# A transformer pair on one core: tiles of the first steps of four stages paired, two sums and a transposition moved, a weight split moved ahead of the first head norm

## The chip, the core and the metric

The kernel runs on one core of one Trainium2 chip (trn2). The metric is the device time of one launch in microseconds (us); a run's time is that of its one core.

## What is computed

The reference chains two blocks over 256 tokens of width 1024, batch 1, one layer each, all in float32. Cut to what matters:

```python
# first block: Mamba-like mixer plus a gated convolution, then a squared-relu MLP
u = rms_norm(x, ln1) * (1 + scale1) + shift1
proj = u @ w_in                     # gates, conv inputs, z, xbc, dt
y = ssd_scan(conv_silu(xbc), softplus(dt), ...) ; y = y * silu(z)
yg = yg * rsqrt(mean(yg * yg) + EPS)            # 8 groups of 256 features
x = x + gate1 * ((sigmoid(gl) * p_conv + sigmoid(gl') * (y @ w_ssm_out)) @ w_o)
u2 = rms_norm(x, ln2) * (1 + scale2) + shift2
x = x + gate2 * (square(relu(u2 @ w_up)) @ w_down)
x = rms_norm(x, final_norm)
# second block: two kinds of attention, then a silu-gated MLP
h = modulate(x); q, k, v = h @ w_in_2 ; q, k = head-wise rms_norm
x = x + g1 * (concat(forget_attention, differential_attention) @ w_out)
x = x + g2 * ((silu(h2 @ w_gate) * (h2 @ w_up)) @ w_down)
```

## The kernel before, in words

The work is a list of 143 steps, numbered from 0, that `plan()` writes down (lines 67 to 152). A step multiplies one weight tile of 1024 rows by 256 columns (8 blocks of 128 rows) with activations that lie transposed in SBUF, features on partitions and 256 tokens in the free dimension. Each weight and each activation is split in a high and a low part, and each product is three matmuls: high by high, high by low, low by high (`product_part`, line 1101). A step has two output blocks of 128 columns, called nb 0 and nb 1, each with a PSUM bank of its own, and so 2 x 8 x 3 = 48 matmuls. Three banks (acc0 to acc2) turn, so that nb 1 of a step takes the bank that nb 0 of the step before it used; a bank is free when VectorE or ScalarE has drained it (`drained`, line 430).

The steps, by kind: xbc 0 to 15, cc/cx/cb 16 to 27, gc/co 28 to 31 and 40 to 43, z 32 to 39, gs/so 44 to 55, wo 56 to 59, up 60 to 75, dn 76 to 91, the attention projections 92 to 104 (dq, dk, fg, dq, dk, fq, fk, fq, fk, dv, dv, fv, fv), o2 105 to 108, gt/u2 109 to 130, d2 131 to 142.

Five engines walk the same list, each with its own loop `for n in range(NS)` and an order written out by hand; they meet through semaphores. The queues around the change:

- **SP** only issues transfers: weight tile n when the low split of tile n-3 is done, and columns of the modulation matrices between them. The change touches none of it.
- **ScalarE** (line 869): at the start of step n it writes the high part of the weight tile of step n+2 (`split_hi`, line 708), then drains banks, squares, takes roots and writes high parts of activations. An inverse root is Ln and Exp, whose function table `log_exp_table` (line 745) loads ahead.
- **VectorE** (line 1534): at the start or the end of a step it writes the low part of a tile, w_lo = raw - w_hi (`split_lo`, line 1377), and drains banks; in the head norms (lines 1671 to 1680) it corrects the root and scales q and k.
- **GpSimd** (line 647): low parts of activations (`lo_part`, line 613), sums of squares (`add_squares`, line 599; the z pairs, line 663), gating.
- **TensorE** (line 1282): the products (`products`, line 1148), and between them the sums of squares over partitions: `x_sum` (line 1048) for the norms of the residual stream, and line 1356 for the z groups; head norms (line 1309), attention scores, transposes (`attn_slot`, line 1227).

Attention work is laid out in slots, two for each step from 92 on: slot 2(n-92)+nb. `S_AT` says in which slot which pair's scores are computed, `T_AT` in which which head's weights are transposed, `PV_AT` where they meet the values:

```python
S_AT = {6: 0, 8: 1, 12: 2, 14: 3, 16: 4, 18: 5, 20: 6, 22: 7}
T_AT = {9: 0, 11: 1, 15: 2, 17: 3, 19: 4, 20: 5, 21: 6, 22: 7, 23: 8, 24: 9, 25: 10, 26: 11}
```

Steps 60 and 109 (and 61, 110 with them) start before the norm ahead of them is known ("late" norms): they multiply unnormed activations, and VectorE scales the result afterwards (lines 1563, 1573). The steps behind them, 62 and 111, use the normed activations as the blocks arrive, of which the last three (N_AHEAD = 5) come late.

Of the kernel before, what the change touches and what calls it, by code (L numbers as in the profile page):

```python
# [193 lines left out]
def build(nc, a, out):  # L194
# [47 lines left out]
    T_AT = {9: 0, 11: 1, 15: 2, 17: 3, 19: 4, 20: 5, 21: 6, 22: 7, 23: 8, 24: 9, 25: 10, 26: 11}  # L242
    PV_AT = {20: (0,), 21: (1,), 22: (2,), 23: (3,), 25: (4, 5), 26: (6, 7), 27: (8, 9), 28: (10, 11)}
    FG = start_of["fg"]
    LO_NB = 1
# [12 lines left out]
    with ExitStack() as ctx, ExitStack() as programs:  # L258
# [186 lines left out]
        SUMS = {0: KB, 1: KB + 1, 2: KB + 2, 4: KB + 3}  # L445
# [9 lines left out]
        def square_used(k):  # L455

            for n, b0, b1 in ((0, 0, KB), (1, KB, 2 * KB), (2, 2 * KB, 4 * KB), (4, 4 * KB, 5 * KB)):
                if b0 <= k < b1:
                    b, x = divmod(k - b0, 2) if n == 2 else (k - b0, 0)
                    if n == 0:  # L460
                        return "xsum_done", b + 1
                    if b == KB - 1:
                        return "xsum_done", SUMS[n]
                    return "sq_added", added_at(n, max(b, 1), x) + 1
# [242 lines left out]
        def _(act):  # L707
# [46 lines left out]
            def x_root(n):  # L754

                act.wait_ge(S("xsum_done"), SUMS[n])
                if n == 2:
                    link(act.activation(mx[:, 0:T], M3[:, T:2 * T], ACT.Ln, bias=eps[:, 1:2], scale=1.0 / D))
                    act.activation(mx[:, 0:T], mx[:, 0:T], ACT.Exp, scale=-0.5).then_inc(S("xroot"), 1)
                    inverse_root(sq[:, 0, :], M4[:, 0:T], D, "xroot")  # L760
# [108 lines left out]
            for n in range(NS):  # L869
# [19 lines left out]
                if zs in (5, 9):  # L889
                    log_exp_table()  # L890
                    act.wait_ge(S("zsum_done"), zs - 1)
                    for bank, _ in Z_BANK[0:2] if zs == 5 else Z_BANK[2:4]:
                        inverse_root(bank[:, :], bank[:, :], 2 * P, "zroot")
# [126 lines left out]
                if n == FG + 2:  # L1020
                    log1p_exp_parts(fgr[:, 1:6, :], fgr[:, 0, :], 1)
                for b in z_blocks(zs):
# [16 lines left out]
        def _(pe):  # L1039
# [7 lines left out]

            def x_sum(n):

                take("M4")  # L1050
                if n == 2:
                    take("M3")
                if n == 0:
                    for i in range(KB):
                        pe.wait_ge(S("xsq"), i + 1)
                        pe.matmul(M4[:, 0:T], ones[:, :], sq[:, i % 4, :], start=(i == 0), stop=(i == KB - 1))\
                          .then_inc(S("xsum_done"), 1)
                else:
# [3 lines left out]
                    if n == 2:  # L1062
                        last_w = sq[:, square_at(n, KB - 1, 1) % 4, :]
                        pe.wait_ge(S("sq_added"), added_at(n, KB - 2, 1) + 1)
                        pe.matmul(M3[:, T:2 * T], ones[:, :], rt[:, 1, :], start=True, stop=False)
                        pe.matmul(M3[:, T:2 * T], eps_ones[:, :], rt[:, 0, :], start=False, stop=False)
                        pe.wait_ge(S("xsq"), square_at(n, KB - 1) + 1)
                        pe.matmul(M3[:, T:2 * T], eps_ones[:, :], last, start=False, stop=False)
                        pe.matmul(M4[:, 0:T], ones[:, :], last, start=False, stop=True)
                        pe.wait_ge(S("xsq"), square_at(n, KB - 1, 1) + 1)  # L1070
                        pe.matmul(M3[:, T:2 * T], ones[:, :], last_w, start=False, stop=True).then_inc(S("xsum_done"), 1)
                    else:
                        pe.wait_ge(S("xsq"), square_at(n, KB - 1) + 1)
                        pe.matmul(M4[:, 0:T], ones[:, :], last, start=False, stop=True).then_inc(S("xsum_done"), 1)
# [205 lines left out]

            jq = 0
            for n in range(NS):
                s = steps[n]
                for nb in range(NB):
                    products(n, nb)
                    if n == SOFT_AT + 2 and nb == 0:
# [60 lines left out]
                zs = n - Z0  # L1347
                if 1 <= zs < 9:
                    g = zs - 1
                    bank, name = Z_BANK[g // 2]  # L1350
                    if g % 2 == 0:
                        take(name)
                    if g in (0, 2):
                        pe.wait_ge(S("exp_done"), HEADS)
                    pe.wait_ge(S("zpair"), zs)
                    pe.matmul(bank[:, g % 2 * T:(g % 2 + 1) * T], ones[:, :], sq[:, 2 * (zs % 2), :], start=True, stop=True)\
                      .then_inc(S("zsum_done"), 1)
                    free[name] = ("f_ready", YS + 4 * (g // 2 + 1))
# [9 lines left out]
        def _(dve):  # L1368
# [165 lines left out]
            for n in range(NS):  # L1534
                s = steps[n]
                if n + 2 < NS and not split_late(n) and s.kind != "xbc" and not adds_tokens(n) and n not in LATE:
# [16 lines left out]
                for nb in range(NB):  # L1553
# [25 lines left out]
                    if s.kind == "xbc":  # L1579
# [11 lines left out]
                        if nb == 0 and n == 2:  # L1591
# [3 lines left out]
                        elif nb == 0:  # L1595
# [46 lines left out]
                    for kind, gate in (("wo", 0), ("dn", 1), ("o2", 2), ("d2", 3)):  # L1642
                        if s.kind == kind and s.last:
# [3 lines left out]
                                                     ALU.add).then_inc(S("x_ready"), 1)  # L1647
                    if s.kind == "up":
# [18 lines left out]
                    prev = steps[n - 1] if n else None  # L1667
                    if nb == 1 and prev and prev.kind in ("dq", "dk", "fq", "fk"):
# [23 lines left out]
                    if split_late(n) and nb == LO_NB:  # L1692
# [85 lines left out]
```

## Time and profile before

| | |
|---|---|
| median of 3 runs | 939.42 us (939.03 to 941.12) |
| the profiled execution's own time | 938.5 us |
| its span | 936.7 us |
| granted TensorE clock, mean over the span | 0.991 |
| PE busy (matmuls) | 896.6 us, 96% |
| DVE (VectorE) busy | 675.7 us, 72% |
| ACT (ScalarE) busy | 543.3 us, 58% |
| POOL (GpSimd) busy | 280.6 us, 30% |
| read from HBM | 200.8 MB, mean 217 GB/s |

PE is TensorE, SPq the queue that issues transfers. Times in a trace are counted from the start of the span. A timeline row has start, duration, engine, line, operation, tiles and count, and in brackets how long the engine had been idle before it and whose result ended that. Matmul rows overlap: one is listed with 0.28 us, but the next starts 0.11 us after it, so stretches are read from starts.

### The profile page before, as it was taken

The numbers are of one execution on the slowest core, as the hardware profiler recorded it, in microseconds if no ns is written. First come the engines' busy times: TensorE is split into PE (matmuls) and PEld (weight loads), VectorE is DVE, ScalarE is ACT, GpSimd is POOL, SyncE is SP. The second block draws the span as 40 slices with busy tenths as digits, with TensorE's granted clock in tenths as the row PEclk, the third lists the DMA queues.
The fourth block names the chain that finished last, engine by engine and source line by source line (L and its number), as shares of the span: only waits on it lengthen the run. The fifth ranks groups of instructions, "written<-read, shape, count | busy, mean of one in ns | idle before, by whom it ended". The sixth has DMA issues, their size and how long they took to land.

```text
span 936.7 us, 17831 instructions
## 1 busy us (share of the span) xinstructions
PE 896.6 (96%) x7390; PEld 864.7 (92%) x7390; DVE 675.7 (72%) x870; ACT 543.3 (58%) x840; POOL 280.6 (30%) x266
## 2 busy tenths in 40 slices
PE   5999999999999999999999999988999889999998
PEld 5899999999998999998999999877888889999998
DVE  5989988887677667848788767678895576755442
ACT  4568655557966764466655444557687674454331
POOL 5500003444377411266654111020003551121100
PEclk9999999999999999999999999999999999999999
DMA  9754555666677578844888887414233348755560
GB/s 366 296 216 155 186 216 200 250 238 252 235 286 258 199 255 297 285 138 150 290 301 291 296 316 282 159 60 166 91 136 133 138 154 300 267 193 200 169 225 23
DMA packets 36112, 203.02 MB, mean 217 GB/s; under 512 B 4928, under 2 KB 6080, under 8 KB 17216
## 3 DMA queue, kind: packets, MB, share of 16 engines
q1 hardware_dynamic: 36032, 201.89, 60.2%
q8 instruction: 58, 0.95, 0.4%
q14 instruction: 22, 0.18, 0.1%
HBM read 200.82 MB, written 1.05 MB: 216 GB/s over the span
## 4 chain that ended last, share of the span: by engine, by line
PE 59%; issue 15%; DVE 12%; ACT 8%; POOL 5%; DMA 1%; SPq 0%; POOLq 0%; ACTq 0%; DVEq 0%
PE acc L1132 53%; ACT w_hi L714 3%; DVE w_lo L1382 2%; DVE ada_w L1440 2%; DVE cv L1585 1%; DMA ada_w<-in_ada_tiles 1%; POOL sq L663 1%; POOL rt L611 1%; POOL ul L617 1%; POOL xs L669 1%; DVE fr L1406 1%; POOL maps L658 1%; PE acc L1097 1%; DVE qk L1680 1%; ACT L994 1%
## 5 line engine op out<-in xcount | busy, mean ns | idle before, releaser
L1382 DVE TENSOR_TENSOR w_lo<-raw,w_hi 128x2048 fp32r<-128x2048 f32 x141 | 322.0, 2284 | 146.8 <-ACT w_hi L714 146.8
L1132 PE MATMUL acc<-uh,w_hi 128*128 128x256 f32 x1320 | 375.5, 285 | 8.0 <-POOL ul L617 5.2
L1132 PE MATMUL acc<-ul,w_hi 128*128 128x256 f32 x1320 | 368.7, 279 | 0.0
L1132 PE MATMUL acc<-uh,w_lo 128*128 128x256 f32 x1320 | 368.7, 279 | 0.0
L714 ACT ACTIVATE w_hi<-raw 128x2048 fp32r<-128x2048 f32 x141 | 266.2, 1888 | 79.7 <-PE acc L1132 79.7
L1132 PEld LDWEIGHTS acc<-uh,w_hi 128*128 128x128 f32 x1320 | 251.3, 190 | 14.6 <-POOL ul L617 5.6
L1132 PEld LDWEIGHTS acc<-ul,w_hi 128*128 128x128 f32 x1320 | 251.0, 190 | 0.4 <-issue 0.2
L1132 PEld LDWEIGHTS acc<-uh,w_lo 128*128 128x128 f32 x1320 | 250.9, 190 | 0.0
L1132 PE MATMUL acc<-hidh,w_hi 128*128 128x256 f32 x432 | 119.2, 276 | 0.0
L1132 PE MATMUL acc<-hidl,w_hi 128*128 128x256 f32 x432 | 119.2, 276 | 0.0
L1132 PE MATMUL acc<-hidh,w_lo 128*128 128x256 f32 x432 | 119.2, 276 | 0.0
L1743 DVE CUSTOM_DVE_ANT_0 colw<-colw,cact,par_all 128x1024 f32<-128x1024 f32 x80 | 116.6, 1464 | 0.4 <-DMA colw<-in_ada_cols 0.4
L617 POOL TENSOR_TENSOR hidl<-fr,hidh 128x256 fp32r<-128x256 f32 x54 | 71.7, 1328 | 122.2 <-ACT hidh L723 122.2
L1132 PEld LDWEIGHTS acc<-hidh,w_hi 128*128 128x128 f32 x432 | 81.1, 188 | 0.0
L1132 PEld LDWEIGHTS acc<-hidl,w_hi 128*128 128x128 f32 x432 | 81.1, 188 | 0.0
L1132 PEld LDWEIGHTS acc<-hidh,w_lo 128*128 128x128 f32 x432 | 81.1, 188 | 0.0
L658 POOL TENSOR_TENSOR maps<-maps 128x384 f32<-128x384 f32 x16 | 21.1, 1317 | 112.8 <-ACT maps L995 112.8
L1585 DVE SCALAR_TENSOR_TENSOR cv<-acc,par_all,cv 128x255 f32<-128x255 f32 (+2 forms) x87 | 41.2, 480 | 4.5 <-ACT cv L915 2.0
L617 POOL TENSOR_TENSOR ycl<-fr,ych 128x256 fp32r<-128x256 f32 x16 | 18.9, 1183 | 83.3 <-ACT ych L723 83.3
L723 ACT ACTIVATE hidh<-fr 128x256 fp32r<-128x256 f32 x54 | 22.2, 411 | 34.3 <-DVE fr L1660 26.9
L1132 PE MATMUL acc<-ych,w_hi 128*128 128x256 f32 x128 | 37.1, 290 | 2.9 <-POOL ycl L617 2.9
L611 POOL TENSOR_TENSOR rt<-rt,sq 128x256 f32<-128x256 f32 x20 | 20.3, 1028 | 60.7 <-ACT sq L742 60.7
(366 smaller groups left out, 1581.0 us busy)
## 6 DMA issues: line engine op xcount, KB each, us to landing
raw<-in_tiles SPq DMA_DIRECT2D x137, 1024.0 KB, 5.2
colw<-in_ada_cols SPq DMA_DIRECT2D x80, 512.0 KB, 5.5
ada_w<-in_ada_tiles SPq DMA_DIRECT2D x8, 1024.0 KB, 17.2
raw<-in_rest SPq DMA_DIRECT2D x4, 768.0 KB, 4.5
cact<-in_c_rows SPq DMA_DIRECT2D x2, 512.0 KB, 4.2
xT<-in_x SPq DMA_DIRECT2D x1, 1024.0 KB, 7.4
first_w<-in_tiles SPq DMA_DIRECT2D x1, 1024.0 KB, 17.2
out<-xT SPq DMA_DIRECT2D x8, 128.0 KB, 3.4
```

The costliest lines, as they stand in the source:

```text
L611: pool.tensor_tensor(rt[:, x, :], first, sq[:, k % 4, :], ALU.add).then_inc(S("sq_added"), 1)
L617: pool.tensor_tensor(lo, uf[:, i, :] if i < YC else fr[:, i % NF, :], hi.bitcast(F32), ALU.subtract).then_inc(S("act_lo"), 1)
L658: pool.tensor_tensor(EXS[q % 4], EXS[q % 4], sc[:, q // 4 % 2, :], ALU.mult).then_inc(S("mul_done"), 1)
L663: pool.tensor_tensor(sq[:, k, :], sq[:, k, :], sq[:, k + 1, :], ALU.add).then_inc(S("zpair"), 1)
L669: pool.tensor_tensor(xs[:, b, :], xs[:, b, :], gt[:, nb, :], ALU.mult).then_inc(S("yz_done"), 1)
L714: act.activation(w_hi[:, n % NHL, 0:s.kts, 0:s.cols], raw_of(n), ACT.Copy)\
L723: act.activation(hi, x, ACT.Copy).then_inc(S("act_hi"), 1)
L1132: ins = pe.matmul(o, l, r, start=(s.k == 0 and i == 0 and not j), stop=(s.last and i == s.kts - 1 and j == 2))
L1382: dve.tensor_tensor(lo, raw_of(n), hi.bitcast(F32), ALU.subtract).then_inc(S("lo_ready"), 1)
L1440: dve.tensor_tensor_reduce(w, w, cact[:, :], 1.0, ada_b[:, c:c + 1], ALU.mult, ALU.add, mod[:, c:c + 1]).then_inc(S("ada_sum"), 1)
L1585: ins = dve.scalar_tensor_tensor(cv[:, i % 2, o:T], ps[:, 0:T - o], ssm_w[:, 32 * tap + fb:32 * tap + fb + 1], cv[:, i % 2, o:T], ALU.mult ...
L1743: dve.tensor_tensor_reduce(w, w, cact[:, :], 1.0, ada_b[:, c:c + 1], ALU.mult, ALU.add, mod[:, c:c + 1]).then_inc(S("col_sum"), 1)
```

## The change

Nine edits. (1) Steps 45, 56, 62 and 111 are "paired": both banks take the first blocks (6, 6, 5 and 5 of them) before either takes the rest. (2) The z group sums on TensorE move from the end of a step to behind nb 0 of the next one, and (3) ScalarE takes the z roots behind the two drains of its step, not ahead of them. (4) Three of the sums of norm 2 move into step 91, ahead of block 6 of nb 1 (`x_sum_ahead`); the sum for ScalarE's first root is finished first and signalled alone. (5) The low split of tile 93 moves on VectorE behind the update of nb 0 in step 91. (6) The low split of tile 95 moves ahead of the first head norm in step 93. (7) Transposition 1 moves from slot 11 to 12. (8) The Ln/Exp table load moves from step 59 to 58 and from 108 to 107. (9) The dt weights' splits move up by one step on ScalarE and by half a step on VectorE.

```diff
-    T_AT = {9: 0, 11: 1, ...
+    T_AT = {9: 0, 12: 1, ...
+    D_LAST = max(n for n in range(NS) if steps[n].kind == "dn")
+    PAIRED = {start_of["wo"]: KB - 2, first["so", 0, 0]: KB - 2, U0 + 2: N_AHEAD, G0 + 2: N_AHEAD}
...
# ScalarE
-                if n == 2:
+                if n == 1:
                     act.wait_ge(S("dt_in"), 16)
                     act.activation(dt_hi[:, :, :], dt_raw[:, :, :], ACT.Copy).then_inc(S("dt_hi"), 1)
-                if (s.kind, s.j) in (("wo", 3), ("dn", 3), ("o2", 3)) and s.last:
+                if (s.kind, s.j) in (("wo", 2), ("dn", 3), ("o2", 2)) and s.last:
                     log_exp_table()
...
-                if zs in (5, 9):           # ahead of the loop over nb
+                if zs in (5, 9):           # behind it
                     log_exp_table()
                     act.wait_ge(S("zsum_done"), zs - 1)
...
# TensorE
+            def x_sum_ahead():
+
+                take("M4")
+                take("M3")
+                pe.wait_ge(S("sq_added"), added_at(2, KB - 2) + 1)
+                pe.matmul(M4[:, 0:T], ones[:, :], rt[:, 0, :], start=True, stop=False)
+                pe.matmul(M3[:, T:2 * T], eps_ones[:, :], rt[:, 0, :], start=True, stop=False)
+                pe.wait_ge(S("sq_added"), added_at(2, KB - 2, 1) + 1)
+                pe.matmul(M3[:, T:2 * T], ones[:, :], rt[:, 1, :], start=False, stop=False)
...
+                elif n in PAIRED:
+                    if nb == 0:
+                        for i0, i1 in ((0, PAIRED[n]), (PAIRED[n], KB)):
+                            for b in range(NB):
+                                for i in range(i0, i1):
+                                    product_part(n, b, i)
                 elif size == 1:
                     for i in range(steps[n].kts):
+                        if n == D_LAST and nb == NB - 1 and i == KB - 2:
+                            x_sum_ahead()
                         product_part(n, nb, i)
...
                     products(n, nb)
+                    if nb == 0 and 2 <= n - Z0 < 10:
+                        z_sum(n - Z0 - 2)
...
# VectorE
-                if n + 2 < NS and not split_late(n) and ... and n not in LATE:
+                if n + 2 < NS and not split_late(n) and ... and n not in LATE and n != D_LAST:
                     split_lo(n + 2)
...
-                        if nb == 0 and n == 2:
+                        if nb == 1 and n == 1:
                             dve.wait_ge(S("dt_hi"), 1)
                             dve.tensor_tensor(dt_lo[:, :, :], ...
...
+                    if n == D_LAST and nb == 0:
+                        split_lo(n + 2)
...
+                    if n == I0 + 1 and nb == LO_NB:
+                        split_lo(n + 2)
                     if nb == 1 and prev and prev.kind in ("dq", "dk", "fq", "fk"):
...
-                    if split_late(n) and nb == LO_NB:
+                    if split_late(n) and n != I0 + 1 and nb == LO_NB:
                         split_lo(n + 2)
```

No instruction is added or removed but for the order: the same sums, splits, products and table loads are issued, and the same transfers.

## Rows read from the trace of the kernel before

**Rows 1.** The page, busy time, share and instructions of each engine.

```profile
PE 896.6 (96%) x7390; PEld 864.7 (92%) x7390; DVE 675.7 (72%) x870; ACT 543.3 (58%) x840; POOL 280.6 (30%) x266
```

**Rows 2.** Waits of PE: who waited, for whom; total us, times, longest us.

```profile
PE m L1356 <- POOL sq L663: 3.4, 2, 2.3
PE m L1061 <- POOL rt L611: 3.1, 2, 2.3
```

**Rows 3.** Windows: us, then busy (instructions) by engine, PEclk, DMA share, GB/s.

```profile
536.06:579.58 43.52, 43.52 (x386) 43.52 (x385) 30.08 (x28) 18.43 (x17) 5.86 (x7) 1.00 0.84 304
297.28:300.69 3.41, 3.41 (x19) 3.41 (x18) 2.70 (x3) 1.89 (x3) 3.41 (x3) 0.50 0.97 381
```

**Rows 4.** Timeline of PE, the instruction behind each idle stretch (445.59: none).

```profile
56.14 0.30 PE L1319 MATMUL m<-uh,dt_hi 128*32 128x256 f32 x1 [1.38 <-DVE dt_lo L1593]
...
83.45 0.36 PE L1132 MATMUL acc<-uh,w_hi 128*128 128x256 f32 x1 [0.58 <-DVE cv L1585]
...
296.16 0.70 PE L1356 MATMUL m<-sq,ones 128*128 128x256 f32 x2 [2.25 <-POOL sq L663]
...
399.12 0.38 PE L1132 MATMUL acc<-ych,w_hi 128*128 128x256 f32 x1 [2.91 <-POOL ycl L617]
...
437.13 0.52 PE L1132 MATMUL acc<-uh,w_hi 128*128 128x256 f32 x1 [1.92 <-POOL ul L617]
...
445.59 0.30 PE L1132 MATMUL acc<-uh,w_hi 128*128 128x256 f32 x1
...
602.28 0.67 PE L1061 MATMUL m<-rt,ones 128*128 128x256 f32 x2 [0.77 <-POOL rt L611]
...
625.32 1.13 PE L1309 MATMUL m<-sq,blk 128*128 128x512 f32 x2 [2.02 <-DVE maps L1671]
...
629.89 0.39 PE L1132 MATMUL acc<-uh,w_hi 128*128 128x256 f32 x1 [2.04 <-DVE w_lo L1382]
...
653.75 0.55 PE L1256 MATMUL m<-ident,cct 128*128 128x128 f32 x3 [2.68 <-DVE cct L1494]
...
763.93 0.39 PE L1132 MATMUL acc<-uh,w_hi 128*128 128x256 f32 x1 [2.48 <-POOL ul L617]
```

**Rows 5.** Timeline of DVE around the dt weights, steps 1 to 3.

```profile
55.67 0.42 DVE L1593 TENSOR_TENSOR dt_lo<-dt_raw,dt_hi 128x256 fp32r<-128x256 f32 x1
...
58.49 1.52 DVE L1585 SCALAR_TENSOR_TENSOR cv<-acc,par_all,cv 128x255 f32<-128x255 f32 x3 [0.98 <-ACT cv L915]
```

**Rows 6.** Timelines of ACT, DVE and POOL around steps 37 and 38.

```profile
284.79 1.28 ACT L747 ACT_TABLE_LOAD   x1
...
292.97 2.56 DVE L1382 TENSOR_TENSOR w_lo<-raw,w_hi 128x2048 fp32r<-128x2048 f32 x1 [2.29 <-ACT w_hi L714]
...
293.62 2.49 POOL L663 TENSOR_TENSOR sq<-sq 128x256 f32<-128x256 f32 x1 [0.24 <-ACT sq L887]
```

**Rows 7.** Timeline of DVE, the drain of step 62.

```profile
445.03 0.75 DVE L1652 TENSOR_TENSOR fr<-acc,gt 128x256 f32<-128x256 f32 x2
```

**Rows 8.** Timelines of DVE, POOL and ACT at the end of step 91.

```profile
598.12 2.29 DVE L1382 TENSOR_TENSOR w_lo<-raw,w_hi 128x2048 fp32r<-128x2048 f32 x1 [1.95 <-ACT w_hi L714]
...
601.41 1.41 POOL L611 TENSOR_TENSOR rt<-rt,sq 128x256 f32<-128x256 f32 x2 [17.95 <-ACT sq L742]
...
605.34 0.47 ACT L758 ACTIVATE mx<-m,eps 128x256 f32<-128x256 f32 x1 [2.46 <-PE m L1071]
```

**Rows 9.** Timeline of DVE in the attention stage, steps 94 to 98.

```profile
631.92 0.88 DVE L1680 SCALAR_TENSOR_TENSOR qk<-qk,par_all,rt 128x256 f32<-128x256 f32 x2
...
652.54 0.25 DVE L1714 COPY dta<-exb 128x16 f32<-128x16 f32 x2
...
661.94 0.55 DVE L1513 SCALAR_TENSOR_TENSOR maps<-dist_ts,m 128x384 f32<-128x384 f32 x1 [1.95 <-PE m L1246]
```

**Rows 10.** Timelines of ACT and POOL around the late norm of step 109.

```profile
746.17 1.28 ACT L747 ACT_TABLE_LOAD   x1
...
761.13 4.12 POOL L617 TENSOR_TENSOR ul<-fr,uh 128x256 fp32r<-128x256 f32 x3 [1.37 <-ACT uh L723]
```

More of the change, by code:

```diff
@@ L1021, in _ @@
                     log1p_exp_parts(fgr[:, 1:6, :], fgr[:, 0, :], 1)
+                if zs in (5, 9):
+                    log_exp_table()
+                    act.wait_ge(S("zsum_done"), zs - 1)
+                    for bank, _ in Z_BANK[0:2] if zs == 5 else Z_BANK[2:4]:
+                        inverse_root(bank[:, :], bank[:, :], 2 * P, "zroot")
                 for b in z_blocks(zs):
@@ L1057, in x_sum @@
                           .then_inc(S("xsum_done"), 1)
+                elif n == 2:
+                    last, last_w = (sq[:, square_at(2, KB - 1, x) % 4, :] for x in range(2))
+                    pe.wait_ge(S("xsq"), square_at(2, KB - 1) + 1)
+                    pe.matmul(M3[:, T:2 * T], eps_ones[:, :], last, start=False, stop=False)
+                    pe.wait_ge(S("xsq"), square_at(2, KB - 1, 1) + 1)
+                    pe.matmul(M3[:, T:2 * T], ones[:, :], last_w, start=False, stop=True).then_inc(S("xsum_done"), 1)
+                    pe.matmul(M4[:, 0:T], ones[:, :], last, start=False, stop=True).then_inc(S("xsum_done"), 1)
                 else:
@@ L1061, in x_sum @@
                     pe.matmul(M4[:, 0:T], ones[:, :], rt[:, 0, :], start=True, stop=False)
[L1062 to L1074, printed above, removed]
+                    pe.wait_ge(S("xsq"), square_at(n, KB - 1) + 1)
+                    pe.matmul(M4[:, 0:T], ones[:, :], last, start=False, stop=True).then_inc(S("xsum_done"), 1)
                 free["M4"] = ("xroot", ROOT[n] + (n == 2))
@@ L1279, in attn_slot, with z_sum @@
                         free["M0"] = ("oroot", c + 1)
+            def z_sum(g):
+                bank, name = Z_BANK[g // 2]
+                if g % 2 == 0:
+                    take(name)
+                if g in (0, 2):
+                    pe.wait_ge(S("exp_done"), HEADS)
+                pe.wait_ge(S("zpair"), g + 1)
+                pe.matmul(bank[:, g % 2 * T:(g % 2 + 1) * T], ones[:, :], sq[:, 2 * ((g + 1) % 2), :], start=True, stop=True)\
+                  .then_inc(S("zsum_done"), 1)
+                free[name] = ("f_ready", YS + 4 * (g // 2 + 1))
             jq = 0
@@ L1346, in _ @@
                         free["M4"] = ("fcum_done", 2)
[L1347 to L1358, printed above, removed]
                 if s.kind == "dn" and s.j == 3 and s.last:
@@ L1535, in _ @@
                 s = steps[n]
-                if n + 2 < NS and not split_late(n) and s.kind != "xbc" and not adds_tokens(n) and n not in LATE:
+                if n + 2 < NS and not split_late(n) and s.kind != "xbc" and not adds_tokens(n) and n not in LATE and n != D_LAST:
                     split_lo(n + 2)
@@ L1594, in _ @@
                                .then_inc(S("dt_lo"), 1)
-                        elif nb == 0:
+                        if nb == 0 and n != 2:
                             split_lo(n + 3 if n < 2 else n + 2)
```

16 lines of the change are left out of this document (6 added, 10 removed).

## The prediction, as put on record before the changed kernel was run

> **What bounds the kernel now.** I read the page's busy line first: TensorE's matmuls cover 896.6 us, 96% of the span, no other engine passes 72% [rows 1]. So nothing a slower engine does counts unless TensorE waits for it. The changed kernel issues the same matmuls; time can come only from two places. One is TensorE's idle stretches, which the view of waits and the timeline name one by one [rows 2, 4]. The other is the clock. In the windows view eight whole up steps (8 x 48 matmuls) take 43.52 us at granted clock 1.00, which is 2.4 GHz: 0.1133 us a matmul, 2.72 us for one output block, 5.44 for a step. In a window of 3.41 us the clock is 0.50, 1.2 GHz [rows 3]: half the work is done, so such a stretch costs 1.7 us. There are five of them, one soon behind each of the stalls that end at 296.16, 399.12, 437.13, 653.75 and 763.93 (2.25, 2.91, 1.92, 2.68, 2.48 us) [rows 4]. Three others of like length (2.02 and 2.04 [rows 4], and the 2.3 us one of the second line of [rows 2]) have none behind them; nor has any stall of 0.6 to 1.4 us. So of eight stalls of 1.9 us or more five were followed by a slow stretch, and I price a stall left at that length with about half of 1.7 us extra.
>
> **Part by part, against the profiled execution** (938.5 us; the median of the runs, 939.4, is 0.9 above it).
>
> *dt weights.* The stall of 1.38 us for dt_lo goes. But step 8 waits for VectorE's convolution chain all the same (0.58 us, for cv), and that chain gets later: the low split (0.42 us) now stands ahead of the convolution of step 2, whose start VectorE awaited 0.98 us [rows 4, 5]. What is gained at 56 us is lost at 64 to 83 us, and about 0.3 more: **-0.3**. Bounds: gain 1.4 (the chain has slack), loss 0.4 (the whole split).
>
> *z sums and roots.* The two z waits are 3.4 us together, the longer 2.3 [rows 2], so the first is 1.15; its sum moves half a step (2.72 us) later and the wait goes. For the second, GpSimd adds the squares at 293.62, 8.83 us after ScalarE's table load at 284.79 began [rows 6]. The roots now start behind the drains, 2.7 us later, but the load of a second table (1.28) and two silus (0.7, my reading) no longer stand inside the path: it takes about 6.9, so the add begins at 294.4, and under w_lo it takes 2.49 us as now. It ends near 296.8. TensorE, which stood there from 293.91 on (296.16 - 2.25), comes 2.72 later, less most of the 1.15, near 295.7, and waits 1.1 in place of 2.25; behind 1.1 us no slow stretch has come. At 296.8 it is at a point that it reached at 296.16 + 2.72 = 298.9 before: 2.1, and 1.7 for the slow stretch, **+3.8**; bounds 2.1 (the slow stretch stays) to 4.2 (two stalls and the stretch less no more than 0.9 of rest).
>
> *wo, step 56.* Both banks take six blocks first. 18 matmuls x 0.1133 = 2.04 of the 2.91 us are covered, 0.9 remains, and the slow stretch goes: 2.04 + 1.7 = **+3.7**; bounds 2.0 (the slow stretch stays) to 3.7. Moving the table load from step 59 to 58 gives 0: the chain of norm 1 begins at the last product of 59, and the load was done by then.
>
> *up, step 62.* 15 matmuls = 1.70 of the 1.92 us would be covered. But nb 1 of step 63 takes the bank of nb 0 of step 62, which VectorE drains from 445.03 on, about 0.4 us of the pair listed [rows 7], and TensorE starts there at 445.59 with no wait [rows 4]. VectorE's drain stands in its queue behind the late norm's work, which doesn't move. If TensorE arrives 1.9 us plus the vanished slow stretch sooner, it stands at that bank for some 2.5 us. The idle time moves from block 5 to step 63: **+0.1**, bounds +0.1 and -1.7 (before, the slow stretch lay under this cover; a new one behind the new stall would not).
>
> *Step 91, three sums and split 93.* In the trace GpSimd adds at 601.41, 0.70 each [rows 8], TensorE waits 0.77, and the root's first operation is at 605.34 [rows 4, 8]. The inputs of the first sum come near 599.3. But the split of tile 93 now starts about there and takes its 2.29 us; GpSimd's adds with VectorE in a split took 2.49 us, without it 0.70 [rows 6, 8]. So held, the first add ends near 602.2, as now, but TensorE waits for it *inside* step 91 from 600.8 on (1.4 us), then does three sums (1.4) and six products (0.7), and the last bank, which the last squares need, is ready at 604.7 and no longer at 601.5; the root comes at 606.9. **-1.5**; bounds +0.35 (GpSimd isn't held) and -1.5. The Trainium skill, "GPSIMD Engine Reference", Key points, has a rule that speaks against this edit: GpSimd shares its SBUF interfaces with VectorE and contends with instructions that have two SBUF inputs, as a split has. By that rule the lower bound holds; by the free add of 0.70 the upper would.
>
> *Split of tile 95.* The w_lo stall of 2.04 us goes, for the split comes before the head norm. But the chain of that norm, through the scaling of q and k at 631.92 (0.88 us for two) [rows 9], is what the scores of slot 6 await, and it gets no earlier; it gets the 2 us of split ahead of it instead. The stall of 2.02 us for the distance maps grows to about 2.5. **+0.15**; bounds +0.4, -0.5.
>
> *Transposition 1.* It waits 2.68 us for cct in slot 11. The next thing in that slot is the forget sums, which wait for VectorE's copies at 652.54, 0.7 us earlier [rows 9]. So the stall falls to 1.95. Behind it VectorE is full, and its only pause is 1.95 us before 661.94 [rows 9]: what TensorE wins beyond that it would wait again. 0.7 or more of stall, the slow stretch's 1.7, capped by 1.95 + 0.2: **+2.1**, bounds 1.3 and 2.4.
>
> *gt, step 111, and the load in step 107.* The load (1.28 us) leaves the path of the root, so what follows, with GpSimd's ul at 761.13, comes 1.28 sooner [rows 10]; pairing covers 1.70. Together 2.98 exceed the 2.48 us stall, and nb 1 of step 112 needs a bank that ScalarE drains early. 2.48 + 1.7 = **+4.2**; bounds 2.5 and 4.4. The 2.3 us stall for rt just before stays: it waits for GpSimd behind a split.
>
> Pairing step 45, with all its blocks there, changes nothing: **0**; what hides it is that both its banks come free over 1 us ahead.
>
> *Sum.* -0.3 + 3.8 + 3.7 + 0.1 - 1.5 + 0.15 + 2.1 + 4.2 = 12.2 off 938.5: 926.3. By the count of stalls above, one slow stretch is likely behind the new 2.5 us stall at step 63 (1.7), and half of one behind the other long ones (0.9): **929.0**. The forecast's own range is 926.3 to 931.5.
>
> **Rivals.** *Stalls pass downstream* at 56 or 111 as at 62: a drain or a low part behind the paired step becomes the bound. For: 62 shows the mechanism. Against: in both, the next bank's drain is early. 933 with one lost, 936.9 with both. Chance 0.18. *Nothing held, no slow stretch:* GpSimd's add in step 91 falls beside no split (+1.8 us) and the 0.50 stretches all go: 924.5 to 926. For: every stall but one or two falls under 2.2 us. Chance 0.12. *z roots behind the drains delay ScalarE's high splits:* w_hi of steps 39 to 41 is 2.7 us later, and w_lo with it; VectorE already awaited w_hi 2.29 us at 292.97 [rows 6]. Then the z gain is lost and 0.7 more: 933.5. Chance 0.08. *Slower:* the clock. The change turns five stalls with a slow stretch into about twelve of 0.9 to 2.5 us. If each of those is followed by 3.41 us at 0.50, it costs 12 x 1.7 = 20.4 on 926.3: 946.7; with eight it is 939.9, level with before. Place: behind steps 38, 56, 63, 91, slots 6 and 11, and the norms. Against: none of the stalls up to 1.4 us had one. Chance 0.04. The Trainium skill, "TensorE: Matmul & The Clock Gate", Part 1, says the gate's observation is free-running, so that one kernel's slow stretches differ from run to run; by that the half-stretches above are a chance, not a rule, and no run here has shown it. *The change doesn't do what it says*: for dt, step 62 and split 95 that is already the forecast.
>
> **Numbers.** Forecast 0.58, the rivals 0.18, 0.12, 0.08 and 0.04. A measurement here tells about 0.2%, 1.9 us, from no change. The range 925.5 to 935.0 takes in the forecast, most of the lucky case, the late z splits and one gain lost downstream; 936.9 and the slower side stay out. Faster than 937.5: 0.91; within: 0.04; slower than 941.3: 0.05.
>
> **What would show it.** Right: a stall of about 1.1 us for sq at the z sums; 0.9 for ycl in step 56; none for ul in 62 but 2.5 for a drain in 63; 1.4 for rt inside step 91 and mx 1.5 us later after it; no w_lo stall at 95 but one for the head norm's qk; about 1.95 in slot 11; none in 111; slow stretches two rather than five. Wrong: more of them than four, a stall in 57 or 112, or VectorE's idle time in steps 94 to 99 larger than before.

## The result, and the profile after

| | before | changed |
|---|---|---|
| median of the first comparison | 939.22 us (936.88 to 941.12, 4 runs) | 927.88 us (927.08 to 930.13, 4 runs) |
| ratio, 95% interval | | 0.9884 (0.9856 to 0.9913) |
| the profiled execution's own time, its span | 938.5, 936.7 | 927.08, 925.3 |
| mean granted clock over the span | 0.991 | 0.996 |

Forecast were 929.0 us, 925.5 to 935.0. A second comparison gave 928.38 us (6 runs), ratio 0.9903 (0.9878 to 0.9928). The first line below is the page's busy line of the changed kernel, to be read against [rows 1].

```profile
PE 890.7 (96%) x7390; PEld 858.2 (93%) x7390; DVE 678.6 (73%) x870; ACT 543.0 (59%) x840; POOL 289.4 (31%) x266
```

The instruction counts are the same. TensorE is busy 5.9 us less with the same matmuls: most of that is half-speed stretches, three fewer at 1.7 us each. GpSimd is busy 8.8 us *more* with the same additions. That is no more work either; it is waiting inside an instruction, which a page counts as busy, and it turns out to be the thread of this case.

The view of waits of the changed kernel, TensorE's own (who waited, for whom; total us, times, longest), answers to [rows 2]:

```profile
PE m L1305 <- POOL sq L665: 2.8, 3, 1.3
PE m L1080 <- POOL rt L613: 2.5, 1, 2.5
PE m L1339 <- DVE maps L1693: 2.4, 1, 2.4
PE acc L1140 <- DVE fr L1672: 2.3, 1, 2.3
PE m L1372 <- DVE dta L1736: 1.8, 1, 1.8
```

And TensorE's timeline of the changed kernel, the instruction behind each idle stretch, answers to [rows 4] (start, duration, engine, line, operation, in brackets the idle time before it and what ended it):

```profile
64.59 0.31 PE L1355 MATMUL m<-ident,gt 32*128 32x32 f32 x2 [1.24 <-ACT gt L1005]
...
297.03 0.48 PE L1305 MATMUL m<-sq,ones 128*128 128x256 f32 x1 [1.27 <-POOL sq L665]
...
311.05 0.48 PE L1305 MATMUL m<-sq,ones 128*128 128x256 f32 x1 [1.09 <-POOL sq L665]
...
396.62 0.38 PE L1140 MATMUL acc<-ych,w_hi 128*128 128x256 f32 x1 [0.87 <-POOL ycl L619]
...
438.56 0.38 PE L1140 MATMUL acc<-uh,w_hi 128*128 128x256 f32 x1 [2.26 <-DVE fr L1672]
...
595.28 0.45 PE L1056 MATMUL m<-rt,ones 128*128 128x256 f32 x1 [1.41 <-POOL rt L613]
...
619.74 0.70 PE L1339 MATMUL m<-sq,blk 128*128 128x512 f32 x1 [2.41 <-DVE maps L1693]
...
646.64 0.28 PE L1372 MATMUL m<-dta,tri 128*128 128x8 f32 x1 [1.78 <-DVE dta L1736]
```

Nothing is left at block 5 of step 111 (2.48 us before), nothing at w_lo of tile 95 (2.04), and step 56 waits 0.87 in place of 2.91. New are 1.24 us for gt in step 5, where the gain on the dt weights goes (step 4 ends 1.15 us sooner, step 5 no sooner), 2.26 at a drain in step 63, 1.41 inside step 91, and 1.09 at a third z sum (step 41). The five half-speed stretches are two, in the windows of the changed kernel (columns as in [rows 3]; the clock is the third number from the end):

```profile
621.24:624.44 3.20, 3.20 (x17) 2.62 (x16) 1.69 (x4) 2.26 (x3) 0.00 (x0) 0.50 0.63 264
648.20:651.83 3.63, 3.63 (x19) 3.63 (x18) 3.50 (x8) 1.15 (x2) 0.00 (x0) 0.53 0.00 0
```

To find where 11.4 us of span went, I took the start of the last matmul of every step in both traces and looked where their difference changes (minus is sooner; "pace" is the time from one matmul to the next at full clock, see the last section):

| steps | change in us | edit and what is in it |
|---|---|---|
| 0 to 33 | +0.2 | dt weights |
| 34 to 41 | -1.8 | z sums and roots |
| 42 to 45, 57 to 59 | -1.5 | the pace of the matmuls; pairing step 45 shows nothing |
| 56 | -3.7 | pairing, and no half-speed stretch |
| 60 to 63 | -0.1 | pairing: 2.65 won in step 62, 2.51 lost in 63 |
| 91, 92 | +0.9 | sums ahead, split 93 (+1.3), pace (-0.4) |
| 93 to 98 | -1.1 | split 95, transposition |
| 99 to 110 | -0.3 | waits and pace |
| 111 to 113 | -4.1 | pairing, table load, no half-speed stretch (-4.5), pace (+0.4) |

### The profile page after: what moved, and what is told of

The parts are those of the page before. It is cut to its first block, busy times and chain, and to the rows that moved or that the text cites. A ratio compares the mean times of both kernels' runs of the same rounds, so it can differ in the third digit from the quotient of the medians.

```text
span 925.3 us, 17831 instructions
## 1 busy us (share of the span) xinstructions
PE 890.7 (96%) x7390; PEld 858.2 (93%) x7390; DVE 678.6 (73%) x870; ACT 543.0 (59%) x840; POOL 289.4 (31%) x266
## 4 chain that ended last, share of the span: by engine, by line
PE 63%; issue 14%; DVE 11%; POOL 5%; ACT 5%; DMA 1%; SPq 0%; ACTq 0%; POOLq 0%; DVEq 0%
PE acc L1140 55%; ACT w_hi L716 2%; DVE w_lo L1400 2%; DVE ada_w L1458 2%; DVE cv L1603 2%; POOL rt L613 1%; DMA ada_w<-in_ada_tiles 1%; PE m L1140 1%; PE m L1225 1%; POOL ysl L619 1%; DVE qk L1702 1%; POOL maps L660 1%; POOL ul L619 1%; PE acc L1105 1%; DVE maps L1696 1%
## 5 line engine op out<-in xcount | busy, mean ns | idle before, releaser
L613 POOL TENSOR_TENSOR rt<-rt,sq 128x256 f32<-128x256 f32 x20 | 23.2, 1173 | 55.5 <-ACT sq L744 55.5
L1664 DVE SCALAR_TENSOR_TENSOR xT<-acc,mod,xT 128x256 f32<-128x256 f32 x31 | 14.4, 480 | 32.0 <-PE acc L1140 32.0
```

Of the source, the lines that this page charges most:

```text
L613: pool.tensor_tensor(rt[:, x, :], first, sq[:, k % 4, :], ALU.add).then_inc(S("sq_added"), 1)
L1664: dve.scalar_tensor_tensor(xT[:, b, :], ps, GATE[gate][:, b:b + 1], xT[:, b, :], ALU.mult, ALU.add).then_inc(S("x_ready"), 1)
```

## The experiments

Twelve kernels were run, each beside the kernel before on its chip; the first seven once each. I read those by the starts of the steps in their traces, which repeat to some 0.1 us where neither a half-speed stretch nor the pace differs, and not by their single times (928.7 to 937.6 us).

**Step 56 paired alone.**

```diff
 kernel before
+    PAIRED = {start_of["wo"]: KB - 2}
```

> The kernel before with step 56 alone paired. My theory: pairing covers 18 matmuls, 2.04 us, so the stall at block 6 falls from 2.91 to about 0.9 and the end of step 56 comes 2.0 us sooner, and 3.7 us sooner if no half-speed stretch follows. The changed kernel showed 3.66 us. A rival reading of those 3.66 us is that the stretch at half speed went by chance and would be back in this run: then 2.0. In either case the time between matmuls in steps 57 to 59, 0.1178 us before, is the open point: if it hangs on what happened in step 56 it is 0.1133 as in the changed kernel, and 0.2 us a step are gained more.

```profile
399.16 0.38 PE L1133 MATMUL acc<-ych,w_hi 128*128 128x256 f32 x1 [0.87 <-POOL ycl L618]
```

The wait is 0.87 and no half-speed stretch follows; step 56 ends 3.66 us sooner, to the hundredth what the changed kernel gained there. Steps 57 to 59 went at 0.1133 us a matmul, for 0.64 us more.

**Step 62 paired alone.**

```diff
 kernel before
+    PAIRED = {U0 + 2: N_AHEAD}
```

> The kernel before with step 62 alone paired. My theory: the stall of 1.92 us for ul goes and comes back in step 63 at its second bank, for VectorE's drain, shortened by nothing: 1.7 to 2.0 us there, the end of step 63 is within 0.3 us of before, apart from the half-speed stretch (1.7 us) that may or may not follow it. Rival: pairing covers 1.7 us for good, and step 63 ends 1.7 us sooner.

```profile
444.66 0.39 PE L1133 MATMUL acc<-uh,w_hi 128*128 128x256 f32 x1 [2.27 <-DVE fr L1659]
```

Step 62 ends 2.34 us sooner and step 63 gives 2.51 back: nothing is won, and no half-speed stretch stands in either step. The wait in step 63 is longer than the 2.0 us expected. The wait has moved from block 5 to the drain that stands behind VectorE's split of tile 64.

**Sums of norm 2 and split 93 back in their old places.**

```diff
 changed kernel
-                        if n == D_LAST and nb == NB - 1 and i == KB - 2:
-                            x_sum_ahead()
-                    if n == D_LAST and nb == 0:
-                        split_lo(n + 2)
... (and `x_sum` does all sums of norm 2 again, as in the kernel before)
```

> The changed kernel with the three sums of norm 2 and the split of tile 93 back in their old places. My theory: these two edits cost 1.3 us (root 1.3 us later in the changed kernel), so without them step 92 starts 1.3 us sooner relative to the end of step 90. Rival (what the edit seems made for): they bring the root forward, and without them it comes later.

The root's first operation (ScalarE's timeline), in this kernel:

```profile
600.88 0.47 ACT L760 ACTIVATE mx<-m,eps 128x256 f32<-128x256 f32 x1 [2.46 <-PE m L1073]
```

and in the changed one:

```profile
599.72 0.47 ACT L760 ACTIVATE mx<-m,eps 128x256 f32<-128x256 f32 x1 [0.82 <-PE m L1075]
```

They must be counted from the start of step 91, which is at 591.44 in the first trace and 588.96 in the second: 9.44 and 10.76 us. The kernel before has 9.44 too (595.90 to 605.34 [rows 8]). The two edits cost 1.32 us at the root, and step 92 starts 1.32 later by the same count (14.50 against 13.18 us).

**Sums ahead, split 93 behind the last update.**

```diff
-                    if n == D_LAST and nb == 0:
+                    if n == D_LAST and nb == NB - 1:
                         split_lo(n + 2)
```

> The changed kernel with the split of tile 93 behind the update of the second half of step 91 and not of the first; the three sums stay ahead. My theory: GpSimd's first addition is held 1.5 us only because VectorE splits beside it. Without a split beside it both additions take 0.7 to 0.75 us each, TensorE waits 0 to 0.3 us in place of 1.41 us, and the root's first operation comes 1.4 to 1.7 us sooner than in the changed kernel. Rival: the additions are long for another reason (their own length, or the squares late), and the wait stays near 1.4 us. If the split then runs late, step 92 starts late: a wait for w_lo of tile 93 would show it.

GpSimd's two additions here (POOL's timeline), with no split beside them:

```profile
595.07 1.42 POOL L613 TENSOR_TENSOR rt<-rt,sq 128x256 f32<-128x256 f32 x2 [16.44 <-ACT sq L744]
```

and in the changed kernel, with VectorE's split beside them:

```profile
592.28 2.28 DVE L1400 TENSOR_TENSOR w_lo<-raw,w_hi 128x2048 fp32r<-128x2048 f32 x1
```

```profile
592.95 2.88 POOL L613 TENSOR_TENSOR rt<-rt,sq 128x256 f32<-128x256 f32 x2 [16.43 <-ACT sq L744]
```

The same two instructions take 1.42 us or 2.88. TensorE's wait of 1.41 us in step 91 is gone, the root comes 9.30 us after the start of step 91 (600.39 - 591.09), and step 92 waits for no w_lo. So the hold explains the loss. The whole trace of the changed kernel says the same: 54 of GpSimd's two-input 128x256 instructions (TENSOR_TENSOR) start while a split runs, and each ends 0.5 to 0.6 us after that split; the 32 with no instruction of VectorE beside them take 0.65 to 0.75 us. This run also shows what the sums ahead are worth when nothing is held: 9.44 - 9.30 = 0.14 us, since TensorE pays for the three sums before its last bank instead of behind it.

**Second table load back in step 108.**

```diff
-                if (s.kind, s.j) in (("wo", 2), ("dn", 3), ("o2", 2)) and s.last:
+                if (s.kind, s.j) in (("wo", 2), ("dn", 3), ("o2", 3)) and s.last:
```

> The changed kernel with the second table load back in step 108 (step 111 stays paired). My theory: the load is worth 1.28 us on the root's path and pairing 1.70 us, and only the sum exceeds the stall of 2.48 us. Without the moved load a stall of 0.8 to 1.2 us for ul is back at block 5 of step 111, and step 111 ends 0.8 to 1.3 us later. Rival: pairing alone covers all, because its second bank starts on blocks that are there; then no stall and no change.

```profile
760.19 0.38 PE L1140 MATMUL acc<-uh,w_hi 128*128 128x256 f32 x1 [0.86 <-POOL ul L619]
```

As expected, 0.86 us is back. Step 111 ends 1.46 later, a little more than the 1.3 expected: blocks 6 and 7 come late too and cost some 0.3 us each. Pairing alone doesn't cover this stall; with the earlier load it does.

**Split of tile 95 back behind the head norm.**

```diff
-                    if n == I0 + 1 and nb == LO_NB:
-                        split_lo(n + 2)
-                    if split_late(n) and n != I0 + 1 and nb == LO_NB:
+                    if split_late(n) and nb == LO_NB:
                         split_lo(n + 2)
```

> The changed kernel with the split of tile 95 back behind the first head norm. My theory: that edit is worth about 0.15 us: the stall of about 2.0 us for w_lo of tile 95 is back, the one for the head norm falls from 2.4 to about 2.0, and the wait for q and k in slot 6 (1.61 us in the run without a half-speed stretch here) goes. The end of step 95 moves by 0.5 us or less, apart from the half-speed stretch. Rival: the edit removed one of two waits for good, and the end of step 95 comes 1.5 to 2 us later without it.

```profile
619.32 0.70 PE L1339 MATMUL m<-sq,blk 128*128 128x512 f32 x1 [2.00 <-DVE maps L1691]
...
623.88 0.39 PE L1140 MATMUL acc<-uh,w_hi 128*128 128x256 f32 x1 [2.06 <-DVE w_lo L1400]
```

Two waits of 2.00 and 2.06 us here; with the edit, in the run with split 93 last, 2.38 for maps and then this one for q and k:

```profile
627.69 0.38 PE L1260 MATMUL m<-qk 64*128 64x128 f32 x2 [1.61 <-DVE qk L1702]
```

4.06 us against 3.99. From the end of step 92 to that of 95 it is 18.46 us here, with a half-speed stretch in step 95, and 16.67 there with none. The kernel before has the two waits of this one and no stretch, and takes 16.80: the edit is worth 0.1 to 0.2, the stretch 1.7. The rival's wait "removed for good" has come out as another wait.

**Transposition 1 back in slot 11.**

```diff
-    T_AT = {9: 0, 12: 1, ...
+    T_AT = {9: 0, 11: 1, ...
```

> The changed kernel with transposition 1 back in slot 11. My theory: TensorE waits 2.5 to 2.7 us for cct there and then nothing for the forget sums, so 0.7 to 0.9 us more stall by the end of step 98; the half-speed stretch is there or not. Rival: VectorE is full up to step 99, so the waits add up to the same and the end of step 99 is within 0.2 us.

```profile
651.26 0.33 PE L1272 MATMUL m<-ident,cct 128*128 128x128 f32 x1 [2.68 <-DVE cct L1512]
```

2.68 us for cct, where the changed kernel has 1.78 for dta; step 98 ends 0.89 later and step 99 0.80, where the rival allowed 0.2. Each of the two has a half-speed stretch behind it.

**Four splits held back or moved.** If splits hold GpSimd, and drains stand behind splits, then four edits on VectorE alone should pay:

```diff
+                if 6 <= n - Z0 < 9:
+                    dve.wait_ge(S("zpair"), n - Z0)
-                ... and n not in LATE and n != D_LAST:
+                ... and n not in LATE and n not in (D_LAST, U0 + 2):
                     split_lo(n + 2)
...
-                    if n == D_LAST and nb == 0:
+                    if n == D_LAST and nb == NB - 1:
                         split_lo(n + 2)
...
+                    if n == U0 + 2 and nb == NB - 1:
+                        split_lo(n + 2)
...
+                if (s.kind, s.j) == ("o2", 3):
+                    dve.wait_ge(S("sq_added"), added_at(4, KB - 2) + 1)
                 if adds_tokens(n):
                     split_lo(n + 2)
```

> The changed kernel with four more edits: VectorE's splits in steps 38 to 40 wait until GpSimd has added the z squares of that step; the split of tile 93 stands behind the last update of step 91; the split of tile 64 stands behind both drains of step 62; the split of tile 110 waits until GpSimd has made the last addition of norm 4. My theory (GpSimd is held by VectorE's splits, and drains stand behind them): the z waits of 1.27, 0.4 and 1.09 us fall to under 0.3 together (2.2 to 2.5 us), 1.4 us less stall in step 91 (1.1 to 1.4 us net), 2.26 us in step 63 falls to under 0.4 (1.9 us), and 2.52 us at the sum of norm 4 falls to 0.7 to 0.9 (1.7 us). In all 6.5 to 7.5 us faster than the changed kernel, near 921. Rivals: the postponed splits make TensorE wait for w_lo in steps 40 to 42, 64 and 110 (waits of 1 us and more with w_lo named), then 3 us or less; or the half-speed stretches take it back.

926.92 us (4 runs), ratio to before 0.9872 (0.9841 to 0.9902): against the changed kernel not to be told apart, and far from the 921 expected. By the trace three of four did what was expected: the wait in step 63 is gone (-1.98 us), steps 91 and 92 have 1.4 us less, and the sum of norm 4 waits 0.70 and not 2.52 (-1.83). But TensorE's and GpSimd's rows show what came of it:

```profile
317.09 0.39 PE L1140 MATMUL acc<-uh,w_hi 128*128 128x256 f32 x1 [1.46 <-DVE mc L1653]
...
752.52 0.38 PE L1140 MATMUL acc<-uh,w_hi 128*128 128x256 f32 x1 [1.68 <-POOL ul L619]
```

```profile
749.73 3.44 POOL L619 TENSOR_TENSOR ul<-fr,uh 128x256 fp32r<-128x256 f32 x2 [1.37 <-ACT uh L725]
```

In steps 38 to 41 1.5 us was won, and 1.8 lost in step 42, for a drain behind the postponed split. And the 1.83 of norm 4 came back in step 111, doubled by a half-speed stretch (3.4 us): the low part of block 5 starts at 749.73 beside the split of tile 112 (from 749.60), and the two low parts take 3.44 us, where 0.75 each would do.

**The changed kernel again, a corrected order, and filled waits**, on one chip:

> The changed kernel again, beside the two below on the same chip: 928 us within 1.5. Its idle stretches are the same to 0.1 us; the half-speed stretches need not be. My theory is that these come only behind idle stretches of TensorE of 1.6 us or more and that chance decides behind which: two to four of them, not all in the places of the first profile (behind the waits in steps 94 and 97). Rival: they are fixed to the places of the first profile.

928.38 us, 926.57 to 932.23. The waits are as before; the half-speed stretches now stand behind the waits in step 63 (2.28 us) and at the sum of norm 4 (2.31), and none is in steps 94 to 99. The rival, fixed places, falls.

```diff
 the kernel with four splits moved
-                if 6 <= n - Z0 < 9:
+                if n - Z0 in (6, 7):
                     dve.wait_ge(S("zpair"), n - Z0)
+                if n == start_of["wo"]:
+                    dve.wait_ge(S("act_lo"), MG + KB)
...
                         x_norm(LATE_NORM[LATE[n] // 2], N_AHEAD, KB)
+                        if s.kind == "gt":
+                            dve.wait_ge(S("act_lo"), U4 + N_AHEAD + 1)
                         split_lo(n + NHL)
```

> The four further edits with three corrections: VectorE waits for GpSimd's z addition only in steps 38 and 39 (in step 40 the wait made its drain late and cost 1.46 us in step 42); the split of tile 58 waits until GpSimd has written the last low part of the activations of step 56; the split of tile 112 waits until GpSimd has written the low part of block 5. My theory, GpSimd held by splits: against the changed kernel 1.3 to 1.7 us less in steps 39 to 42, 0.87 in step 56, 2.0 in step 63, 1.1 in steps 91 and 92, 1.8 at the sum of norm 4, and the 1.68 us wait that came back in step 111 of the run with four edits stays under 0.3: 7 to 7.5 us, near 921, if as many half-speed stretches come. Rival: what is gained at the sum of norm 4 comes back in step 111 or 112 by another wait, as it did in that run (3.4 us with the half-speed stretch): then near 924.

```profile
310.68 0.61 PE L1305 MATMUL m<-sq,ones 128*128 128x256 f32 x1 [2.43 <-POOL sq L665]
...
754.46 0.45 PE L1140 MATMUL acc<-uh,w_hi 128*128 128x256 f32 x1 [2.06 <-POOL ul L619]
```

926.16 us, ratio 0.9875 (0.9849 to 0.9901), not the 921 expected. Step 56 has no wait left (-1.16 with what follows), as expected. But without the wait in step 40 the z addition of that step is held, for a wait of 2.43 us, and the split of 112, let go after block 5, now holds block 6: 2.06. Both corrections moved the hold by one instruction. Its trace has four half-speed stretches, two of them behind these waits, and the clock is 0.993 to 0.996 in its six runs.

```diff
 the kernel above
+            def fill(count):
+                take("M4")
+                for _ in range(count):
+                    pe.matmul(M4[:, 0:T], ones[:, :], tri[:, :], start=True, stop=True)
...
+                    if nb == 0 and n == FG:
+                        fill(5)
...
+                    if n == FG + 1 and nb == 0:
+                        fill(3)
...
+                        fill(3)
                         pe.wait_ge(S("nlf_done"), 1)
```

> The same with 11 extra products of constants (0.43 us each, into a bank that is rewritten before it is read) ahead of the three long waits that are left in the attention stage: 5 in step 94, 3 ahead of the scores in slot 6, 3 ahead of the forget sums. They compute nothing that is used. My theory, a half-speed stretch needs TensorE idle before it: with the waits filled to under 0.5 us each there is none in steps 94 to 99 in any run, and the clock over the span is 0.998 or more; the time falls by 1.7 us for each stretch that the kernel without them has there, and by nothing where it has none. Rival: the clock doesn't hang on these waits, and stretches come there as before; or the extra products delay the scores by up to 0.6 us where they outlast the wait.

924.20 us (923.65 to 926.01, 5 runs), ratio 0.9857 (0.9833 to 0.9881), 2.0 us under the kernel without them on the same chip (924.56 to 928.23). The clock is 0.996 to 0.998 in the five runs, one of them under the 0.998 expected; in the trace there is no stretch in steps 94 to 99, where the unfilled kernel has two. The filled kernel ends step 94 1.65 us sooner and the second half of step 95 at the same time (628.37 against 628.30): there TensorE must wait for q and k in any case, so that a half-speed stretch in step 94 costs nothing. The one in step 98 costs 1.4. The trace gives one more stretch less, in step 111 (from the end of step 109 to that of 112 19.51 us against 20.87), and that is not the work of the fills: none stands there, and the wait before it is 2.24 us, so it was chance. The wait of 2.43 us in step 41 isn't filled either and has a stretch behind it in both.

**The last order.** The z waits are left out, the split of tile 112 waits for all three late blocks, and the fills stay:

```diff
-                if n - Z0 in (6, 7):
-                    dve.wait_ge(S("zpair"), n - Z0)
...
-                            dve.wait_ge(S("act_lo"), U4 + N_AHEAD + 1)
+                            dve.wait_ge(S("act_lo"), U4 + KB)
```

> The kernel with the extra products, without the waits for the z additions, and with the split of tile 112 held back until GpSimd has written all three late blocks (in the two runs before, it started between blocks 5 and 6, and GpSimd's low part of block 6 took 2.85 us beside it, for a wait of 2.06 and 2.24 us in step 111). My theory: steps 39 to 42 are as in the changed kernel (two waits of 1.27 and 1.1 to 1.3 us, 1.4 us less than with the waits for z) and no half-speed stretch there; the wait in step 111 is under 0.3 us, and 0.5 to 1 us comes back in step 112 as a wait for w_lo of that tile, since the split ends near 1.5 us later. In all 2 to 3.5 us less than 924.2: 921 to 922. Rival: VectorE's drains behind the split of 112 are late in turn, and all of the 2.2 us comes back in steps 112 and 113: then 922.5 to 924.

922.18 us (921.88 to 923.41, 5 runs), ratio to before 0.9815 (0.9792 to 0.9838), the best of all. It ran on another chip than the two kernels before it, and the intervals of the ratios overlap by a little, so the step from 924.20 is less sure than each kernel's gain on the kernel before. Spans and clocks of the last three:

```profile
core 0: 924.8 us, clock 0.993
```

```profile
core 0: 922.5 us, clock 0.998
```

```profile
core 0: 921.4 us, clock 1.000
```

The clock is 1.000 in all five of its runs; behind the first 40 us of its trace TensorE has no wait over 1.27 us. GpSimd's three low parts take 2.23 us in all, and step 111 has no wait. The rival was right about what comes next, though: it is a drain behind the late split, and nearly all comes back.

```profile
749.00 2.23 POOL L619 TENSOR_TENSOR ul<-fr,uh 128x256 fp32r<-128x256 f32 x3 [1.37 <-ACT uh L725]
```

```profile
754.04 0.36 PE L1146 MATMUL acc<-uh,w_hi 128*128 128x256 f32 x1 [1.10 <-DVE stg L1606]
```

From step 109's end to 112's it is 19.18 us, 19.51 in the kernel before it. So this correction gave 0.3 us. Leaving the z stage alone gave 0.9 in steps 34 to 42, one half-speed stretch less included, and a slower pace took 0.6 back in steps 43 to 45. A quicker pace between steps 64 and 92 gave another 0.7. The two spans differ by 1.1 us, the medians by 2.0; the rest is not seen in one trace of each.

## Why the prediction was right, and where it was not

The sum was made against the profiled execution, 938.5 us: 9.5 off, to 929.0. The changed kernel's own is 927.08, 11.4 off.

| term | forecast | measured | shown by |
|---|---|---|---|
| dt weights | -0.3 | -0.2 | step starts alone |
| z sums and roots | +3.8 | +1.8 | step starts alone; two later waits |
| wo, step 56 | +3.7 | +3.7 | alone: 3.66 |
| up, step 62 | +0.1 | +0.1 | alone: -0.2 |
| step 91, split 93 | -1.5 | -1.3 | undone: 1.32 |
| split of tile 95 | +0.15 | +0.2 | undone: 0.1 to 0.2 besides a stretch |
| transposition 1 | +2.1 | +0.9 | undone: 0.89 |
| gt, step 111 | +4.2 | +4.5 | load undone: 1.46 of it lost |
| half-speed stretches left over | -2.6 | 0 beside the terms | one in the row of transposition 1, one free |
| pace of the matmuls | not foreseen | +1.5 | the same code in another run |

Right, as put on record: the stall of step 62 returns in step 63 (2.26 us, "some 2.5"); the wait in step 91 is 1.41 us ("1.4") and the root 1.3 later ("1.5"); step 56 keeps 0.87 ("0.9"); in slot 11 1.78 is left ("1.95"); step 111 has none; the split before the head norm only changes which wait TensorE stands in. The wait for q and k that was foreseen is hidden in the first trace of the changed kernel, under a half-speed stretch, and stands open in the five later traces that have the moved split but neither fills nor a stretch there (1.61 to 1.70 us). VectorE's idle time from the end of step 93 to that of 99, a sign of being wrong if it grew, fell from 9.5 to 8.1 us.

*The z term was mis-sized by half.* The step was that at the second sum TensorE "waits 1.1 in place of 2.25", and for that one sum it held: the addition started at 294.21 (forecast 294.4) and ended at 296.98 (296.8), as GpSimd's row shows, and the wait was 1.27.

```profile
294.21 2.77 POOL L665 TENSOR_TENSOR sq<-sq 128x256 f32<-128x256 f32 x1
...
299.31 3.49 POOL L619 TENSOR_TENSOR ysl<-fr,ysh 128x256 fp32r<-128x256 f32 x2
...
309.28 1.72 POOL L665 TENSOR_TENSOR sq<-sq 128x256 f32<-128x256 f32 x1
```

```profile
293.58 2.81 DVE L1400 TENSOR_TENSOR w_lo<-raw,w_hi 128x2048 fp32r<-128x2048 f32 x1
...
299.47 2.74 DVE L1400 TENSOR_TENSOR w_lo<-raw,w_hi 128x2048 fp32r<-128x2048 f32 x1 [0.71 <-ACT w_hi L716]
...
308.73 1.68 DVE L1765 CUSTOM_DVE_ANT_0 colw<-colw,cact,par_all 128x1024 f32<-128x1024 f32 x1
```

By the end of step 39 3.7 us were won, as forecast. But the step stopped there, and steps 40 and 41 gave 1.85 back. GpSimd's rows stand in the order of its program, and VectorE goes on holding what stands in front of the next sum: the low parts at 299.31 beside a split, for a wait of 0.45 us in step 40, and then low parts beside a split and the addition at 309.28 beside VectorE's product of a modulation column, for one of 1.09 in step 41. So it isn't the splits alone that hold GpSimd. No run undid the z edits by themselves. A stage whose helper is late has to be followed to its end, not to its first sum.

*The transposition's term took a half-speed stretch as gone that its own count left at one in two.* Of 2.1 us, 0.7 or more was the stall, and 0.9 was measured. The rest was the stretch, and with 1.78 us of wait left (1.95 forecast) it came here too. Two stretches came where 1.5 were forecast, but one lies in this term already and the other was free, so nothing of the 2.6 us set aside for them shows beside the terms. The closeness of 929.0 to 927.9 is in part luck: 2.0 and 1.2 us too much (z, transposition) stand against 2.6 and 1.5 too little (stretches, pace).

*The stretches.* All 14 traces of this case, waits of TensorE by length (behind the first 40 us) and how many had a half-speed stretch begin within the next 4 us:

| idle before | waits | followed by a stretch |
|---|---|---|
| 0.5 to 1.5 us | 137 | 0 |
| 1.5 to 1.9 | 15 | 7 |
| 1.9 to 2.2 | 12 | 4 |
| 2.2 to 2.9 | 40 | 22 |

The price put on a stall left at 1.9 us or more, "about half of 1.7 us extra", was right in its count, 26 of 52. But shorter waits have stretches too: the shortest with one behind it is 1.68 us. And three of the 33 stretches, in the traces of three variants and all behind the wait in step 98, lasted 6.83 us and not 3.41, which costs twice as much. The Trainium skill, "TensorE: Matmul & The Clock Gate", Part 1, calls the gate's observation free-running; the runs agree: the changed kernel's stretches stood in other places in its second trace, and its clock went between 0.993 and 0.998 in its ten runs. In the kernel before, runs at 0.987 took 940.6 us (mean of 9) and runs at 0.993 took 936.9 (8): 3.7 us of a spread of 8.3 (933.6 to 941.9 in 28 runs).

*GpSimd under VectorE.* The rule of the Trainium skill, "GPSIMD Engine Reference", Key points (shared SBUF interfaces, contention with instructions of two SBUF inputs) was weighed against the edit in step 91. The trace agrees: the additions took 2.88 us beside a split and 1.42 without, so the bound of that rule was the one that held.

The slower rival (a stretch behind each of twelve waits) fell on the same count: none followed a wait under 1.5 us. Stalls passing downstream, the second rival, was not true of steps 56 and 111 in the changed kernel, but it is just what met the versions that I made to beat it.

## What to carry to other kernels

Pairing two banks over the blocks that are there pays the covered matmuls in full where the next bank is free (step 56), and nothing where it is drained behind a weight split (step 62): look at the drain before the pairing. In these traces a GpSimd instruction that starts beside a long VectorE subtraction ends only 0.6 us after it, so place GpSimd's work that TensorE waits for between the splits, and follow what the moved split stands in front of. Bring TensorE's waits under 1.5 us or fill them with products that are thrown away: both together gave the granted clock 1.000 in all five runs of the last kernel and narrowed its times to 1.5 us. What the last order would give without the fills was not run.

## What the runs showed that was not expected

At full granted clock the same 128x256 products start either every 0.1133 us, for tens of steps on end, or every 0.1178, for up to eight (38 to 45 of the last kernel): 0.2 us a step. The windows view shows it as records in 5 us: first in steps 57 and 58 of the kernel before, then in the same steps with step 56 paired alone.

```profile
410.00:415.00 5.00, 5.00 (x45) 5.00 (x44) 4.55 (x5) 3.44 (x6) 3.85 (x2) 1.00 0.28 72
```

```profile
406.00:411.00 5.00, 5.00 (x47) 5.00 (x46) 4.73 (x5) 3.27 (x5) 4.36 (x3) 1.00 0.25 61
```

It isn't the code: in the second run of the changed kernel steps 57 to 59 went at 0.1178 again, in its first at 0.1133; and they went at 0.1133 with step 62 alone paired, which changes nothing before them. The pace changes at waits, at other kinds of products and at half-speed stretches, and then holds for a while. Between the first two traces it was worth 1.5 us of the 11.4. What sets it was not tried, and stays open.

The wait for dt_lo in step 3 (1.38 us before) is gone in five of the eleven traces with the dt edit, is 0.23 to 0.58 us in five and 0.88 in the last kernel's, though these kernels differ in nothing before it. Why was not looked into.
